# Three heads' probabilities weighed one round later in the attention stage of a one-core decoder step

## What is computed

```python
def diff_attn_core(q, k, v, qpos, kpos, rel_bias, lam):
    s = einsum('bqhmd,bkhmd->bhmqk', q, k2) * (QK_HEAD_DIM ** -0.5)
    s = where(dist >= 0, s + bias[None, :, None], NEG_INF)
    p = softmax(s, axis=-1)
    a = p[:, :, 0] - lam * p[:, :, 1]
    return einsum('bhqk,bkhd->bqhd', a.astype(v.dtype), v)

def diff_head_out(o, subln_gain, lam_init):
    o = rmsnorm(o, subln_gain, SUBLN_EPS) * (1.0 - lam_init)
```

## Time and profile before

| | us |
|---|---|
| median of three runs | 1327.81 (1327.78 to 1327.84) |
| profiled execution, its time | 1327.47 |
| its span, first to last instruction | 1325.70 |
| PE busy | 1311.2 (99%) |
| DVE busy | 727.5 (55%) |
| ACT busy | 446.9 (34%) |
| POOL busy | 157.1 (12%) |

### The profile page before, as it was taken

The page is one execution under the profiler, slowest core; times in us unless marked ns, Lnnn a source line. Parts: engine busy times, 40 slices in busy tenths (PEclk is TensorE's granted clock), DMA queues, the critical chain, the costliest instruction groups (busy, mean ns, idle before and its releaser), DMA issues.

```text
span 1325.7 us, 21954 instructions
## 1 busy us (share of the span) xinstructions
PE 1311.2 (99%) x8364; PEld 1190.1 (90%) x8364; DVE 727.5 (55%) x1185; ACT 446.9 (34%) x764; POOL 157.1 (12%) x323
## 2 busy tenths in 40 slices
PE   8999999999999999999999999999999999999998
PEld 7999999977667888998989898999989898989986
DVE  6446754268886655556453545455354636453556
ACT  6312001057777443441322232232313131323332
POOL 2027000022222211200000000000000000000003
PEclk9999999999999999999999999999999999999999
DMA  7777888367786241420111102010202011020117
GB/s 243 228 233 226 264 247 191 102 220 243 242 267 215 93 142 49 120 80 17 63 32 54 41 16 79 16 63 16 79 16 75 20 63 32 26 69 16 48 49 139
DMA packets 145737, 146.97 MB, mean 111 GB/s; under 512 B 26876, under 2 KB 118693, under 8 KB 145669
## 3 DMA queue, kind: packets, MB, share of 16 engines
q1 hardware_dynamic: 107353, 122.30, 28.7%
q10 hardware_dynamic: 37324, 20.24, 5.6%
q0 software_dynamic: 992, 3.54, 1.6%
HBM read 114.06 MB, written 31.47 MB: 110 GB/s over the span
## 4 chain that ended last, share of the span: by engine, by line
PE 94%; ACT 1%; DVE 1%; issue 1%; POOL 1%; DMA 0%; SPq 0%; POOLq 0%; DVEq 0%; ACTq 0%
PE PS L2521 40%; PE PS L2239 18%; PE PS L2586 17%; PE PS L2465 7%; PE PS L2289 2%; PE PS L2601 2%; PE PS L2616 2%; PE PS L2329 1%; PE PS L2316 1%; PE PS L2392 1%; PE PS L2362 1%; PE PS L2224 1%; PE PS L2456 1%; PE PS L2372 1%; ACT prob L1102 1%
## 5 line engine op out<-in xcount | busy, mean ns | idle before, releaser
L2521 PE MATMUL PS<-act_lo,wu_hi 128*128 128x364 f32 (+1 forms) x1056 | 346.4, 328 | 0.0
L2521 PE MATMUL PS<-act_hi,wu_lo 128*128 128x364 f32 (+1 forms) x1056 | 346.0, 328 | 0.0
L2521 PE MATMUL PS<-act_hi,wu_hi 128*128 128x364 f32 (+1 forms) x1056 | 345.9, 328 | 0.0
L2521 PEld LDWEIGHTS PS<-act_hi,wu_hi 128*128 128x128 f32 x1056 | 198.5, 188 | 0.5
L2521 PEld LDWEIGHTS PS<-act_lo,wu_hi 128*128 128x128 f32 x1056 | 198.1, 188 | 0.4
L2521 PEld LDWEIGHTS PS<-act_hi,wu_lo 128*128 128x128 f32 x1056 | 198.3, 188 | 0.0
L2004 DVE TENSOR_TENSOR y_acc<-y_acc,PS 128x512 f32<-128x512 f32 x162 | 111.2, 687 | 116.0 <-PE PS L2586 116.0
L2586 PE MATMUL PS<-wd_hi,g_hi 128*128 128x512 f32 x324 | 130.1, 402 | 0.0
L2586 PE MATMUL PS<-wd_lo,g_hi 128*128 128x512 f32 x324 | 128.0, 395 | 0.0
L2586 PE MATMUL PS<-wd_hi,g_lo 128*128 128x512 f32 x288 | 114.0, 396 | 0.0
L1364 ACT CAST g_hi<-conv 128x1088 fp32r<-128x1088 f32 x21 | 23.2, 1103 | 245.7 <-PE PS L2586 189.7
(11 more groups left out here) (294 smaller groups left out, 2293.9 us busy)
## 6 DMA issues: line engine op xcount, KB each, us to landing
wu_raw<-in_w_up_dram SPq DMA_DIRECT2D x44, 512.0 KB, 3.9
k_tok<-in_cache_k_dram SPq DMA_DIRECT2D x64, 256.0 KB, 3.9
keys_t<-k_turned ACTq DMA_DIRECT2D x128, 128.0 KB, 3.6
vpage<-in_cache_v_dram SPq DMA_DIRECT2D x64, 256.0 KB, 3.5
wd_raw<-in_w_down_dram SPq DMA_DIRECT2D x22, 512.0 KB, 5.3
w_raw<-in_w_in_dram SPq DMA_DIRECT2D x20, 512.0 KB, 6.6
kt_mid<-keys_t SPq DMA_DIRECT2D x10, 512.0 KB, 5.1
kt_b<-keys_t SPq DMA_DIRECT2D x10, 512.0 KB, 5.8
```

Of the source, the lines that this page charges most:

```text
L2521: mm = nc.tensor.matmul(PS[:, 3 * half + c, 0:kept(c)], a[:, half, k, :], b[:, k, KEPT[c]], start=(j == 0), stop=(j == len(parts) - 1))
```

## The change

The weigh of a round of the first three heads stands one round later on PE: in round s, behind the second turn, PE weighs round s - 2 and no longer round s - 1. `take_rows`, `out_norm`, `turn_out` and `take_out` of these rounds move with it by one round. `LATE` is 15, the first round of the last head, and `CATCH` is 16: in round 16 PE weighs round 14 right behind the first turn, ahead of the sample scores, and round 15 at the old place; from there on all is as before. `precip` gets eight places in place of four, so that a mix needs not wait for the factor of a step whose rows are now normed later. The sample scores stay where they were, between the two turns. No instruction is added or taken away, on any engine.

```diff
-    precip = small[:, 128:136].rearrange("p (i m) -> p i m", m=2)
+    precip = stat[:, 104:120].rearrange("p (i m) -> p i m", m=2)
...
-    TURN_OUT = {ROUND_OF[subs[-1]] + 2: g for g, subs in enumerate(OUT_SETS[:6])}
+    TURN_OUT = {ROUND_OF[subs[-1]] + 3: g for g, subs in enumerate(OUT_SETS[:6])}
+    LATE = (H - 1) * RIN
+    CATCH = LATE + 1
+    def weighed_at(s):
+        return [r for r in range(len(ROUNDS) - 1) if (r + 2 if r < LATE else r + 1) == s]
+    def normed_at(s):
+        return [r for r in range(len(ROUNDS)) if (r + 3 if r < LATE else r + 2) == s]
...
+            if s == CATCH:
+                take_rows(ROUNDS[LATE - 1])
...
-            if s >= 1:
-                take_rows(before)
+            if weighed_at(s):
+                take_rows(ROUNDS[weighed_at(s)[-1]])
...
-            if i >= 4:
-                dve.wait_ge(ofac_ready, i - 3)
-            nc.vector.reciprocal(precip[:, i % 4, :], prob_sum[:, i % 4, :]).then_inc(dve_step, 1)
+            if i >= 8:
+                dve.wait_ge(ofac_ready, i - 7)
+            nc.vector.reciprocal(precip[:, i % 8, :], prob_sum[:, i % 4, :]).then_inc(dve_step, 1)
...
-            for i in ROUNDS[s - 2] if s >= 2 else ():
-                out_norm(i)
+            for r in normed_at(s):
+                for i in ROUNDS[r]:
+                    out_norm(i)
...
+            if s == CATCH:
+                for i in ROUNDS[LATE - 1]:
+                    weigh(i)
             for j in SMP_JOBS[s]:
                 smp_scores(j)
...
             if len(before) == 2:
                 turn(before[1])
-            for i in before:
-                weigh(i)
-                if i == NSTEP - 4:
-                    turn_out(6)
+            if 2 <= s < CATCH:
+                for i in ROUNDS[s - 2]:
+                    weigh(i)
+            if s >= CATCH:
+                for i in before:
+                    weigh(i)
+                    if i == NSTEP - 4:
+                        turn_out(6)
```

More of the change, by code:

```diff
@@ L1130, in take_rows @@
                     act.wait_ge(osq_ready, i)
+                if i >= 4:
+                    act.wait_ge(ofac_ready, i - 3)
                 nc.scalar.activation(o_sq[:], o_nrm[:, i % QB, :], ACT.Square,
-                                     scale=precip[:, i % 4, 0:1], accum_out=o_ssq[:, i % 4:i % 4 + 1]).then_inc(osq_ready, 1)
+                                     scale=precip[:, i % 8, 0:1], accum_out=o_ssq[:, i % 4:i % 4 + 1]).then_inc(osq_ready, 1)
         def take_out(g):
@@ L1500, in _ @@
                 pool.wait_ge(onrm_ready, i - 3)
-            nc.gpsimd.tensor_tensor(o_fac[:, c], o_rstd[:, c], precip[:, i % 4, 0:1], ALU.mult).then_inc(ofac_ready, 1)
+            nc.gpsimd.tensor_tensor(o_fac[:, c], o_rstd[:, c], precip[:, i % 8, 0:1], ALU.mult).then_inc(ofac_ready, 1)
         pool.wait_ge(sscore_ready, 4 * NB)
@@ L1675, in mix @@
             dve.wait_ge(prob_ready, 2 * i + 2)
-            if i >= 4:
-                dve.wait_ge(ofac_ready, i - 3)
-            nc.vector.reciprocal(precip[:, i % 4, :], prob_sum[:, i % 4, :]).then_inc(dve_step, 1)
+            if i >= 8:
+                dve.wait_ge(ofac_ready, i - 7)
+            nc.vector.reciprocal(precip[:, i % 8, :], prob_sum[:, i % 4, :]).then_inc(dve_step, 1)
             own_step(dve, dve_step)
-            nc.vector.scalar_tensor_tensor(pcoef[:, i % 4:i % 4 + 1], precip[:, i % 4, 1:2], neg_lam,
+            nc.vector.scalar_tensor_tensor(pcoef[:, i % 4:i % 4 + 1], precip[:, i % 8, 1:2], neg_lam,
                                            prob_sum[:, i % 4, 0:1], ALU.mult, ALU.mult).then_inc(dve_step, 1)
```

## The result

The changed kernel takes 1330.08 us (1329.78 to 1330.54, 19 runs) against 1327.77 (1327.24 to 1328.07, 19 runs, the first three of which gave the 1327.81 of the prediction): a ratio of 1.0018, 95% interval 1.0011 to 1.0025, or 2.3 us more. That is just under the predicted range and within 0.2% of before, where rival B stood (+2.1).

A forecast was written before the change was run, and what follows sets the result against it. No engine is near full; PE, ACT and DVE wait for each other in a ring without the weighs. Terms 1.0 + 1.3 + 1.9 + 0.5 = 4.7 us gave a median of 1332.5, range 1330.2 to 1334.0.

The forecast's parts named there:

- rival B: Within 0.2%: PE's shorter weigh in rounds 7 and 12 covers most of DVE's late norms; +2.1, 1329.9; chance 0.10.
- The start: Round 2: without the weigh of step 0, PE's scores start earlier, a lag of -0.3 that carries on.
- the ring: Scores on PE, minima on DVE, exponents on ACT freeing banks for next scores, mixes on DVE releasing turns; weighs stand outside.
- ACT, rounds 5 and 6: Two steps' rows and a copy of four ahead of exponents make round 7's scores late, lag +0.5.
- DVE, rounds 6 and 11: Late norms wait for ACT's squares and POOL, delaying factors, mixes and turns: +1.0 at round 8, then +1.3; the largest term.
- POOL's 0.95: First POOL instruction of steps 5, 13 and 21, taken as bound to the instruction and expected again; otherwise 0.76 less per head.
- the low sum: Total if POOL's long instructions don't come again: 3.2 us rather than 4.7.
- The catch-up: Round 16: two weighs of width 8 on PE, with ACT's rows waiting for the added one; +1.4 to +1.9, taken as +1.9.
- Round 17: A `turn_out` of 0.53 comes in on PE with no wait to hide it: +0.5.
- The eight places: Eight places of `precip`: no instruction more, and mixes don't wait for factors now a round later; no cost.
- A: Rival, faster: the weighs' waits were on the path, 5.1 us go and 1.9 comes back; 3.2 faster, 1324.6; chance 0.05.
- C: Rival, much slower: lag collides with the next stage, 0.28 in twelve rounds; 3.4 more, 1336.1; chance 0.04.

## Why the prediction was wrong

*The start (-0.3): right*, -0.27. It didn't last, though I had said that the ring carries it on: in round 4 PE's second scores wait for ACT again, and at round 5 the lag is +0.08.

*ACT, rounds 5 and 6 (+0.5 at the scores of round 7): the size holds, the cause is only half.* The lag grew by 0.7 from round 5 to 7, where the forecast had 0.8 (from -0.3 to +0.5). Beside ACT's later exponents, PE's own round 6 is longer by 4 blocks less a `turn_out`; I had counted the shorter weigh of round 7, but not the longer one of round 6. In the changed kernel PE's own work ends at 313.89 - 0.15 = 313.74 and ACT's exponents at 313.83, 0.61 and 0.70 behind 313.13, so each end alone would give nearly this lag. The run with `take_out` moved doesn't separate them, since it adds a `turn_out` to PE in that round.

*DVE, rounds 6 and 11 (1.0 and 1.3): the step that failed.* The forecast was that the first turn of round 7 is late by all of DVE's delay, 1.6, with POOL's 0.95 in it, and that +1.0 is left at round 8 and 1.3 more at round 13. Measured: the turn is 0.93 late, +0.14 is left at round 8 (+0.06 against round 5), and +0.1 comes in from round 10 to 13, so round 13 is 0.21 late and not 2.3, which I had named as a sign of being wrong. Four things were mis-sized.

- POOL's 0.95, taken as bound to step 5, is 0.76 too much; it is a wait for DVE's mix, and the step moved away from that mix. POOL needs 2.15 for the two steps (310.88 to 312.84 + 0.19) and not 2.98. But the squares come off ACT 0.4 later than forecast, as the lead is gone, so the samples' factors are only 0.37 earlier than forecast (313.33, not 313.7). I had named the 0.95 as the doubt and gave the low sum for it, 3.2, but chose the other since it came every eighth step; it did so because every eighth step met a mix 1024 columns wide.
- The turn at 315.05 did not wait for its mix, as I had read it: the mix had ended 0.36 before, and the turn followed the scores. So a part of DVE's delay falls into that time, and most of what is left at the turn is the scores' own lateness (0.76), which I had already counted. The late norms add about 0.15, as the run with the norms behind the mixes shows.
- For the second head I added 0.3, since the lead would be gone, but it was gone after round 4, so both heads behave alike.
- Round 7 gives back 0.79, not 0.6.

*The catch-up (1.9): right in size*, 1.77, and so is its working: PE's own work ends at 386.55 and ACT's exponents at 386.45 (386.25 + 0.20), so the two ends meet there. What makes it more than the exchange on PE (1.89 less 0.53) is 0.33 at the turn, where PE waits for the mix (0.27) and for the bank of the second half; the working had 0 to 0.5 for that bank. With the weigh cut to one block 0.4 of it remains, ACT's rows ahead of the exponents.

*Round 17 (+0.5): right*, 0.45.

*The eight places (0): right.*

*The rivals.* A fell: the weighs' wait went and nothing got faster, not even with the norms behind the mixes (+1.92). B came out in size, and mainly for the reason that it gave: the shorter weigh of round 7 makes up for the head's lateness. But that lateness is mostly the scores', not the norms', and the 0.3 of the start, which B kept, was lost, so its +2.1 is a little lucky. Its chance should have been larger, since its condition and the short-POOL bound of my own sum lay within a microsecond of each other. C fell (its own sum gives 1335.9, not 1336.1).

So the loss is not in the rounds that wait for POOL. It is that PE's work was taken out of rounds in which it then waits for ACT (0.27 won for a weigh of 1.1) and put into one that has no time to spare (2.2 paid in rounds 16 and 17, of which 0.45 is the `turn_out` that moved with it).

## What to carry to other kernels

Where two engines take turns and end nearly together, work moved from one round to another rarely comes out even: price the removal by what is late next, and the addition in full, unless the trace shows a wait just there and nothing else hangs on the moved work. Here weighs that were moved gave 0.3 to 1.4 at first, and putting them back cost 1.2 to 2.2; of work only added or only cut, 0.0 to 1.78 was paid and 0.0 to 0.54 gained. And before a long instance of a short instruction is tied to its place in the code, look at what the other engines run at that moment, and compare the two ends.

## What was not expected of the hardware

POOL's 128x1 instruction took 0.95 beside a DVE mix of 128x1024 and 0.19 beside the same mix in quarters. PE's granted clock fell to 0.50 for some 3 us after a wait of 1.46 at 294.85, though waits of 1.34 and 1.46 at other places (302.98 in the changed kernel, 302.89 with `take_out` moved) left it at 1.00; what tells them apart no run here shows. And a DVE instruction whose inputs were ready started 0.30 late in a certain place of its code; why just there no run shows.
